# Work at both joints between stages moved ahead, the last norm's scaling over two steps, and scores ahead of turns in the chunk steps of grouped attention

## The reference

```python
def reference(x, c, ctx, ...):
    for i in range(2):                       # layer 0: grouped attention, layer 1: neighbourhood attention
        h  = rms_norm(x,   norm_g[i]) * (1 + scale)   + shift
        hc = rms_norm(ctx, norm_g[i]) * (1 + scale_c) + shift_c
        y, yc = mixer(h, hc, ...)            # yc in layer 0 only
        x = x + gate * y
        ctx = ctx + gate_c * yc
    return rms_norm(x, final_g)

def gqa_axial_mixer(...):                    # 8 heads of 128, K and V shared by groups of heads
    q, k, v, g = split(h @ w_in)             # q and k normed, rotary on latent tokens
    o = softmax(q @ k.T * 128 ** -0.5) @ v   # latent queries: 1280 keys; context queries: the 256 context keys
    return (o * silu(g)) @ w_out

def neighbourhood_mixer(...):                # 16 heads of 64
    s_loc = q_row @ k_window.T * 64 ** -0.5 + bias      # 8 x 16 window around each token
    s_ctx = q_row @ k_c.T * 64 ** -0.5                  # and the 256 context keys
    o = softmax([s_loc, s_ctx]) @ [v_window, v_c]
    return (o * silu(g)) @ w_out
```

## Time and profile before

| | us |
|---|---|
| median of 3 runs | 1543.13 (1537.99 to 1545.09) |
| profiled execution | 1539.14 |
| its span | 1537.3 |
| TensorE matmul busy | 1486.0 (97%) |
| VectorE busy | 989.3 (64%) |
| ScalarE busy | 809.4 (53%) |
| GpSimd busy | 419.6 (27%) |

### The profile page before, as it was taken

How to read it: one execution, slowest core, us unless ns; L and a number is a source line. 1 busy time by engine, 2 the same in 40 slices (tenths; PEclk the granted TensorE clock), 3 DMA queues, 4 the chain that set the end, 5 groups by cost and what they waited for, 6 DMA issues and landing times. The chain is left out here.

```text
span 1537.3 us, 26346 instructions
## 1 busy us (share of the span) xinstructions
PE 1486.0 (97%) x9387; PEld 1300.1 (85%) x9387; DVE 989.3 (64%) x2099; ACT 809.4 (53%) x1848; POOL 419.6 (27%) x513
## 2 busy tenths in 40 slices
PE   6999999999999999989999999999997999999998
PEld 3688788897998899978888888889997889989996
DVE  5665636427888888853448966576221987778883
ACT  7422321127777777755554433344112887777772
POOL 2322101002222111100122333220490453454541
PEclk9999999999999999999999999999998999999999
DMA  9435425405333433347663344479857999999882
GB/s 361 162 121 155 134 83 179 159 19 148 69 64 64 71 45 41 42 109 227 201 204 115 126 158 137 149 211 282 276 137 225 298 300 271 261 264 270 258 235 68
DMA packets 207174, 257.53 MB, mean 168 GB/s; under 512 B 39378, under 2 KB 168996, under 8 KB 207012
## 3 DMA queue, kind: packets, MB, share of 16 engines
q1 hardware_dynamic: 204596, 247.45, 55.8%
q10 hardware_dynamic: 2448, 8.39, 1.9%
HBM read 192.83 MB, written 78.80 MB: 177 GB/s over the span
## 5 line engine op out<-in xcount | busy, mean ns | idle before, releaser
L1222 ACT ACTIVATE prob<-S,nm,qk_inv 128x512 f32<-128x512 f32 (+1 forms) x208 | 146.5, 708 | 3.5 <-DVE nm L1155 3.5
L600 PE MATMUL pp<-h_hi,w_hi 128*128 128x512 f32 (+1 forms) x408 | 147.5, 362 | 0.0
L601 PE MATMUL pp<-h_lo,w_hi 128*128 128x512 f32 (+1 forms) x408 | 144.5, 354 | 0.0
L602 PE MATMUL pp<-h_hi,w_lo 128*128 128x512 f32 (+1 forms) x408 | 144.4, 354 | 0.0
L2624 DVE CUSTOM_DVE_ANT_0 nprob<-nS,bias_set 128x640 f32<-128x640 f32 x128 | 105.1, 821 | 58.5 <-PE nS L2456 36.5
L1175 DVE TENSOR_TENSOR ptlo<-TB,pthi 128x512 fp32r<-128x512 f32 (+1 forms) x192 | 114.7, 598 | 35.3 <-ACT pthi L1234 35.0
L2542 ACT CAST npt_hi<-nTB 128x256 fp32r<-128x256 f32 (+1 forms) x256 | 103.1, 425 | 56.9 <-PE nTB L2467 50.6
L1234 ACT CAST pthi<-TB 128x512 fp32r<-128x512 f32 (+1 forms) x192 | 99.4, 518 | 57.9 <-PE TB L1104 57.9
L1148 DVE TENSOR_REDUCE mx<-S 128x1 f32<-128x512 f32 (+1 forms) x208 | 117.7, 581 | 10.8 <-PE S L1096 9.4
L2639 DVE TENSOR_TENSOR npt_lo<-nTB,npt_hi 128x256 fp32r<-128x256 f32 (+1 forms) x256 | 115.0, 483 | 5.1 <-ACT npt_hi L2542 3.9
L2533 ACT ACTIVATE nprob<-nprob,selector 128x640 f32<-128x640 f32 x128 | 106.5, 832 | 15.4 <-issue 8.9
(11 more groups left out here) (325 smaller groups left out, 4442.8 us busy)
## 6 DMA issues: line engine op xcount, KB each, us to landing
kq_scratch<-p_stage SPq DMA_DIRECT2D x96, 256.0 KB, 3.9
keys<-kq_scratch SPq DMA_DIRECT2D x32, 768.0 KB, 4.9
bias_set<-bias_scratch SPq DMA_DIRECT2D x64, 384.0 KB, 6.3
v_strip<-v_scratch SPq DMA_DIRECT2D x128, 128.0 KB, 5.3
wearly<-in_mod_w SPq DMA_DIRECT2D x15, 1024.0 KB, 7.0
bias_scratch<-bias_wide_scratch SPq DMA_DIRECT2D x16, 768.0 KB, 6.5
w_raw<-in_na_w_in SPq DMA_DIRECT2D x11, 1024.0 KB, 6.1
wside<-in_mod_w SPq DMA_DIRECT2D x9, 1024.0 KB, 7.2
```

Of the source, the lines that this page charges most:

```text
L600: pe.matmul(acc, whi[:, k, ws], hi[:, k, a:a + width], start=(k == 0), stop=False)
L601: pe.matmul(acc, whi[:, k, ws], lo[:, k, a:a + width], start=False, stop=False)
L602: last = pe.matmul(acc, wlo[:, k, ws], hi[:, k, a:a + width], start=False, stop=(k == KT - 1))
L1222: act.activation(prob[:, p % 5, a:a + n], S[:, score_bank(p, k), 0:n], ACT.Exp, bias=nm[:, p % 5:p % 5 + 1], scale=q_scale(h - 1, p) if p ...
```

## The change

It has four parts.

1. In grouped attention TensorE takes in each chunk step first `scores`, then `turn`, then `product`. The order on ScalarE and VectorE stays.
2. First joint: the casts `o_high` of the first two tiles and their `o_low` are done in the tail of `grouped_attention`, at its steps 0 and 1 on ScalarE, 1 and 2 on VectorE, each behind the gating of its tiles. For this `o_hi` and `o_lo` get a place of their own, across both blocks.
3. Second joint: SyncE leaves the block without waiting for the last stores of v (`c.last_stores`); the last stage waits for them behind its first loads, and GpSimd ahead of the second memset. `prob` is placed ahead of the gates and bias sets in memory. The last stage is entered with `clear_first=False`: the semaphores of the block before are cleared at the kernel's end. The table for Exp is loaded on ScalarE ahead of the joint.
4. Last stage: `finish` of a tile is split, one half at step p-5, the other at p-6, and the store and the load of x for tiles below LATE are issued by SyncE (`tile_out`, `tile_in`), behind the gate's load of unit 4 x tile + 14.

```diff
-            def _(pool):
-                for sem in old:
+                for sem in old if clear_first else []:
                     pool.sem_clear(sem)
...
                         for k in range(3):
+                            if k < len(chunks):
+                                scores(h, kv, p, k)
                             if k < len(turns):
                                 turn(h, q, k)
-                            if k < len(chunks):
-                                scores(h, kv, p, k)
                             if live(gr, prev, tail):
...
+                        if tail and 1 <= p < 3:
+                            dve.wait_ge(o_high, p)
+                            dve.tensor_tensor(o_lo[:, :, first_tokens(p - 1)], qk[:, :, first_tokens(p - 1)],
+                                              o_hi[:, p - 1, :, :], ALU.subtract).then_inc(o_low, 1)
...
+                        if tail and p < 2:
+                            act.wait_ge(qkd, QH * CHUNKS)
+                            act.wait_ge(gated, (QH - 1) * GQA_GROUPS + 1)
+                            act.copy(o_hi[:, p, :, :], qk[:, :, first_tokens(p)]).then_inc(o_high, 1)
...
-                for i in range(3):
-                    sp.wait_ge(vst[i], v_stored_by(VB * TT + (i - VB * TT) % 3))
                 sp.wait_ge(early, 80)
+                c.last_stores = [(vst[i], v_stored_by(VB * TT + (i - VB * TT) % 3)) for i in range(3)]
...
                 def step(n):
-                    pe.wait_ge(old, n + 1)
                     if n >= 2:
+                        pe.wait_ge(old, n - 1)
                         pe.wait_ge(td, n - 1)
...
-                o_high(0)
                 gate_row(0)
                 for k in range(4):
                     w_high(k)
-                o_high(1)
...
+                    if u == 3 * TT:
+                        act.activation(consts["silu_cols"][:, 0:1], consts["eps"][:, :], ACT.Exp)
...
-        with c.block() as block:
+        with c.block(clear_first=False) as block:
...
+                def tile_out(tile):
+                    sp.wait_ge(outd, 2 * tile + 2)
+                    sp.dma_start(tile_rows(io["out"][0], tile), work[:, :]).then_inc(st, 16)
+
+                def tile_in(tile):
+                    sp.dma_start(x_of(tile), tile_rows(io["x1"], tile)).then_inc(xl, 16)
...
                         kq_in(u + 1)
+                        if u == 0:
+                            for stored, count in c.last_stores:
+                                sp.wait_ge(stored, count)
                         bias_in(2 * u + 2)
                     v_in(u)
...
                     gate_in(u)
+                    tile, rest = divmod(u - 14, 4)
+                    if rest == 0 and 0 <= tile < LATE:
+                        tile_out(tile)
+                        tile_in(tile + 1)
...
-                            finish(done[0])
-                    done = o_step(p - 5)
-                    if done and done[1] == 1 and done[2] == PAIRS - 1 and done[0] < LATE:
-                        if done[0] == 0:
-                            dve.wait_ge(gl, 16)
-                        finish(done[0])
+                            finish(done[0], range(2))
+                    for b in range(2):
+                        done = o_step(p - 5 - b)
+                        if done and done[1] == 1 and done[2] == PAIRS - 1 and done[0] < LATE:
+                            if done[0] == 0 and b == 0:
+                                dve.wait_ge(gl, 16)
+                            finish(done[0], [b])
...
                 for i in range(1, SETS):
+                    if i == 2:
+                        for stored, count in c.last_stores:
+                            pool.wait_ge(stored, count)
                     pool.memset(bias[i][:, :, 0:NCTX], 0.0).then_inc(zero, 1)
...
+                pool.wait_ge(old, UNITS)
+                for sem in c.old_sems:
+                    pool.sem_clear(sem)
```

More of the change, by code:

```diff
@@ L122, in block @@
     @contextmanager
-    def block(self):
+    def block(self, clear_first=True):
         with self.nc.Block() as block:
@@ L1361, in keys_before, with out_and_second_projections @@
     return sum(kind == "k" for kind, _ in PAIRS2[:j])
-def out_and_second_projections(c, io, consts, mod, qk, hi, lo, wa, w1, keys, bias0, w_out, w, w_out1):
+def out_and_second_projections(c, io, consts, mod, qk, hi, lo, wa, w1, keys, bias0, o_hi, o_lo, w_out, w, w_out1):
     nc = c.nc
@@ L1388, in out_and_second_projections @@
         h_unused, lo_raw = c.sb("h_hi_raw", [P, KT, T]), c.sb("h_lo_raw", [P, KT, T])
-    with c.scope((80, 120)):
-        o_lo = c.sb("o_lo", [P, KT, T], F32R)
     with c.scope((80, 120)):
@@ L2594, in _ @@
                         norm(done[0])
-                    for later in (4, 6):
-                        done = o_step(p - later)
-                        if not (done and done[1] == 1 and done[2] == PAIRS - 1 and (later == 4) == (done[0] >= LATE)):
-                            continue
+                    done = o_step(p - 4)
+                    if done and done[1] == 1 and done[2] == PAIRS - 1 and done[0] >= LATE:
                         x_out(done[0])
-                        if done[0] + 1 < TILES - 2:
-                            x_in(done[0] + 1)
                     if p == STEPS + 1:
@@ L2672, in finish @@
                         dve.wait_ge(lated, tile - LATE + 1)
-                    for b in range(2):
+                    for b in bs:
                         cols = slice(512 * b, 512 * b + 512)
@@ L2812, in backbone @@
             wbuf = c.sb("w_raw", [P, KT, 256]), c.sb("w_hi", [P, KT, 256], F32R), c.sb("w_lo", [P, KT, 256], F32R)
+        with c.scope((152, 160)):
+            o_hi = c.sb("o_hi", [P, 2, KT, P], F32R)
+        with c.scope((80, 120)):
+            o_lo = c.sb("o_lo", [P, KT, T], F32R)
         with c.scope((160, 170)):
```

24 lines of the change are left out of this document (12 added, 12 removed).

## The result

| | us | against before |
|---|---|---|
| kernel before, median of 4 runs | 1541.53 (1537.99 to 1545.09) | |
| changed kernel, median of 4 runs | 1556.94 (1556.45 to 1557.66) | ratio 1.0106, 95% interval 1.009 to 1.0123 |
| profiled executions | 1539.14 before, 1557.34 after | +18.2 |

The changed kernel is slower by more than 0.5%, as forecast, and lies in the range; it is 3.4 us above the predicted 1553.5.

What follows compares the result with a forecast made beforehand. TensorE works nearly everywhere, so only its waits count. Parts of +15, 0, -2 and -2.4 sum to +10.6 us, giving 1549.7 on the profiled 1539.1 and a forecast of 1553.5 on the 1543.1 median; range 1544.5 to 1562.

Steps and rivals of the forecast that it cites:

- S(1,2): Scores of query tile 1, chunk step 2 of a head: TensorE waits 0.33 us, the chain from the turn being 1.60.
- S(3,2): Scores of query tile 3, chunk step 2: wait 0.56 us for the exponential that frees their bank, chain 2.04 against 1.48.
- S(4,0): Scores of query tile 4, chunk step 0: reach exponential (2,1) 0.22 us early and wait that long.
- S(4,2): Scores of query tile 4, chunk step 2: wait 0.56 us for the exponential, by the same 2.04 chain as step 3.
- S(5,0): Scores of query tile 5, chunk step 0: reach exponential (3,1) 0.22 us early and wait that long.
- S(5,2): Scores of query tile 5, chunk step 2: wait 0.12 us, since chunk step 1 has only one product block.
- S(7,2): Scores of query tile 7, chunk step 2: wait 0.12 us, since chunk step 1 has only one product block.
- step 9: Step 9 of a head: S(9,0), formerly in the shadow of a 2.12 us chain, now lies ahead of it, costing 0.36.
- +1.7: Last stage from its fourth step: if TensorE's clock rises when it did, 3.5 us more dense work runs at half rate.
- rival (c): Second joint: TensorE's clock keeps its upper level through the shorter gap, -5.5 to -6.5 instead of -2, 1549.5 us; chance 0.15.
- the term that I put at +0.5: Last stage: the later-issued load of x may land late and delay TensorE, +0.5 us for all tiles.
- Rival (b): Last stage: load of x still takes 9.1 us and is late, +15 for part 4's +0.5, 1567 us; chance 0.10.

Runs made afterwards that it cites:

- ahead_only: Kernel before with only TensorE's scores put ahead of turns in each chunk step of grouped attention; 1559.85 us, ratio 1.0125.
- after_again: The changed kernel profiled once more without any edit; S(0) to S(4) 9.65 us, S(4) to S(40) 78.22 us.
- clear_only: Kernel before with only GpSimd's 101 semaphore clears moved from the second joint to the kernel's end; 1541.85 us in one run.
- rest_only: Changed kernel with part 1 undone, turns ahead of scores again; 1536.22 us, ratio 0.9974 against the kernel before.
- before_again: The kernel before profiled once more without any edit; S(0) to S(4) 11.32 us, S(4) to S(40) 79.80 us.
- x_halves: Changed kernel without part 1, with the load of the next x tile cut into two half-row loads; 1532.72 us, ratio 0.9951 against before.
- split_act_queue: Changed kernel without part 1, with the finished tile's store and next load of x issued by ScalarE again; 1557.16 us, ratio 1.0106.

## Why the prediction was right, and where not

**Part 1** was forecast at +15 with bounds 10 and 18 and is +19.2 (the trace of the changed kernel, and ahead_only). The mechanism is the one described, place by place (waits in us of a steady head):

| | S(1,2) | S(3,2) | S(4,0) | S(4,2) | S(5,0) | S(5,2) | S(7,2) |
|---|---|---|---|---|---|---|---|
| forecast | 0.33 | 0.56 | 0.22 | 0.56 | 0.22 | 0.12 | 0.12 |
| measured | 0.31 | 0.56 | 0.30 | 0.56 | 0.21 | 0.11 | 0.13 |

Head 0 costs 1.98, where I took 2. Too small was the sum for a steady head, 1.85 for 2.45. The waits are 0.18 more than summed, most of it in step 9, which costs 0.49 where 0.36 was forecast: T(9,2) waits 0.67 for 0.29, T(9,1) 0.08 and S(9,0) 0.05 that weren't there. Most of the rest, some 0.4, is what I named and put into the upper bound only: matmuls right behind a wait. In the rows above, scores of 512 keys take 0.47 from the first to the third matmul when they follow products (484.00 to 484.47) and 0.54 behind a wait (488.08 to 488.62); scores of 256 keys hold TensorE 0.36 and 0.46. It is paid wherever TensorE stops, five or six times a head; I should have summed it, not bounded it. So the upper bound of 18 was too low as well.

**Part 2**, forecast at 0, bounds -0.4 and +0.5: by the delays in the table of places, from the last product (+19.2) to the last stores of v (+18.9), it comes out within them, -0.3. The same stretch differs by up to 2 us between traces that don't differ there, and no run has this part by itself, so the sign isn't shown. The wait of 0.39 for o_lo is gone:

```profile
699.53 1.94 PE L1734 MATMUL p<-ident,mod 128*128 128x128 f32 x8 [5.43 <-PEq L127]
701.13 0.78 PE L1760 MATMUL p<-w_out_hi_a,o_hi 128*128 128x512 f32 x1
```

From the gate rows to the projection it is 1.60 (2.33 before): 0.73 shorter, not 0.39, since the bracket of the earlier trace rows counts from a modelled end. The loss of up to 0.44 at ScalarE's first cast didn't show as a delay: VectorE's last multiplication with the sums starts 4.0 us behind the last product before (674.59, 678.59) and 4.1 after (693.82, 697.89). Of the 0.7 won, 0.3 goes back, it seems by a way that I had named at the second joint only: TensorE's clock is at 0.50 there for 6.8 us in both traces (from 678.8 before, from 698.2 after), and of the projections 3.1 us lie in it before and 3.9 after; 0.8 us more at 0.50 would be an estimated 0.3 to 0.4.

**Part 3**, forecast at -2 with -3.5 by the fourth step and +1.7 given back where the clock is granted at 0.50. By S(4) it is -4.0 in the changed kernel (18.9 to 14.9) and -3.2 in after_again. S(0) comes 0.69 behind SyncE's last issue where it came 2.24 behind the earlier trace rows, and the second memset waits for the stores as described, without making anyone wait:

```profile
1177.30 21.38 SPq L1645 DMA_DIRECT2D v_scratch<-v_stage  x16
```

```profile
1199.33 0.53 POOL L2728 MEMSET bias_set<- 128x512 f32 x1 [29.29 <-POOLq L127]
1200.50 0.53 POOL L2728 MEMSET bias_set<- 128x512 f32 x1 [0.64 <-DMA v_scratch<-v_stage]
```

The step that failed is the clock. It rose 7.4 us behind S(0) and not 12.1 as before, as in part of rival (c). The granted clock in two stretches of the changed kernel (columns as in the earlier trace rows, PEclk is the third from the end):

```profile
1200.00:1206.50 6.50, 4.65 (x17) 3.36 (x16) 2.91 (x8) 2.59 (x7) 1.74 (x3) 0.50 0.84 282
1207.00:1213.00 6.00, 5.00 (x39) 4.46 (x38) 4.93 (x16) 4.83 (x13) 0.58 (x2) 1.00 1.03 351
```

It is granted at 0.50 for 6.8 us (1200.0 to 1206.8) where it was for 13.7 (1180.5 to 1194.2). The +1.7 takes that for half the rate and half the frequency, which no run shows; granted 0.50, scores of 256 columns start 0.21 us apart in the kernel before (1187.13 and 1187.34), granted 1.00 0.12 (1195.92 and 1196.04), so I estimate that 3.5 us of such work lose 1.5. The stretch is 10.2 us in clear_only and after_again, 6.8 or 10.2 in the traces built on rest_only, and 13.7 or 17.1 in those with both waits of before. clear_only separates the two edits: without the clears the 11.30 us are 1.66 less, as forecast; the 8.88 of the changed kernel is 0.8 less than that, it seems by the clock, and its second execution has 9.65. How much of the 4.0 survives can't be read from one pair of traces, since the next stretch varies by 3 between executions. By all of them, from SyncE's first of the last stores of v to S(40), the five with the old joint take 111.8 to 114.9 us (mean 113.3) and the seven with the new one 108.2 to 114.9 (mean 109.9): some -3.4 for the -2 forecast, by means of values that scatter as much. No run has the stores' wait by itself.

**Part 4**, forecast at -2.4, gave nothing: S(40) to the end takes 258.3 to 259.6 in the six traces of the table that have the old last stage there and 258.1, 259.6 and 260.0 in the three that have the new one (rest_only, the changed kernel twice), +0.3 by the means. The gain is there: 0.58 at each of five tiles, and it is VectorE's alone. In before_again ScalarE issued that load in 0.62 us, not 1.68, and S(58) to S(59) took 3.35 all the same (1320.92 to 1324.27). The load of x has taken it back, the term that I put at +0.5 on an estimate that no row of before showed: it comes to +3.4 in the changed kernel and +2.0 in rest_only, against the steps of x_halves and less the 0.8 that the load cost before. It took 6.7 to 7.8, not under 5.7 and not 9.1, and is 0.9 to 1.1 late at four tiles and 1.96 at the last:

```profile
1512.03 0.69 DVE L2672 TENSOR_TENSOR x_strip<-nacc,x_strip 128x512 f32<-128x512 f32 x1 [1.96 <-DMA x_strip<-x_scratch]
```

At four tiles TensorE loses 0.56 to 0.76, at the last 1.6, where the next step had nothing to spare either. x_halves takes exactly this away and is worth 3.5 against rest_only. Rival (b) had the right place; its load of 9.1 was that of ScalarE's queue, and split_act_queue shows what such a load costs: TensorE waits 15.3, near the 15 of the rival, and an estimated 7 to 8 more go to the clock at the stops, which it left out.

**Parts 2 to 4 together** were forecast at -4.4; rest_only gives -4.5 on the medians, but by other sizes: the second joint better than forecast, as far as the scatter lets one tell, the scaling worse. That the sum agrees is luck. The sum with part 1 is +14.7, the changed kernel's medians say +15.4. That its profiled execution lies 18.2 above that of before comes for 2.9 from S(4) to S(40), in which the first profile of before was the shortest of all. The median of 1543.1 on which I forecast was that of three runs; later ones put it at 1540.2 to 1541.5. That base, 2 too high, and the better second joint hid part of what part 1 (4 more) and part 4 (3 more) cost; that the forecast is only 3.4 off is luck to that extent. (10.6 on 1543.1 is 1553.7; the 1553.5 on record is a slip without weight.)

The grouped attention's tail has six steps, not seven as the section on the kernel says, and `x_in` behind a finished tile loads the next tile of x, not the next but one; nothing above rests on either.

**A version that beats both** is x_halves: parts 2 to 4 without part 1, with the load of x in halves, 0.5% below the kernel before and, by the two ratios, 1.5% below the changed one.

## What to carry to other kernels

When one engine's order is changed and its partner's isn't, follow one chain through both lists: here the scores, moved ahead of the turn, waited for an exponential that stood behind the cast of that same turn. Swapping the partner's order as well only moves the wait on, if the partner used its old order to fill a wait of its own (1.51 us for the maximum). A wait costs more than its length: scores behind one took 0.54 us for 0.47, and with stops of 3.0 to 4.4 us TensorE's granted clock fell to 0.50, by my estimate a third of the 22 us of split_act_queue. And a load that reuses a buffer is worth cutting where the buffer comes free piece by piece: 3.5 us here.

## What was not expected of the hardware

- A load of x of 512 KB behind a finished tile took 6.2 to 7.8 us on SyncE's queue (fifteen loads, three traces) and 7.0 to 11.3 on ScalarE's (thirty-five, seven traces). In a stretch of 3.5 us with both queues busy, each had half of the engines' time (51.8% and 51.3%).
- Each of four stops of TensorE of 3.0 to 4.4 us in the midst of dense work came with 3.4 or 6.8 us at a granted clock of 0.50, from within it or from 0.5 to 1.2 us behind it (split_act_queue); the fifth, of 0.8, brought none.
- S(4) to S(40) of the last stage took the same kernel 3.0 us longer in one execution than in the next, and up to 6.5 between kernels that don't differ there (76.84 and 83.33), by the clock and by loads of v, while the heads of attention repeated within 0.1.
